# A gated encoder block on one core: the latent columns move from plain groups of pieces to block products, and three one-tile gate pieces stand beside each attention head

## The reference, cut to what matters

```python
u = rmsnorm(x, g_mix)
z = u @ w_in      # columns: qa 1024 | ka 256 | va 256 | cq 512 | ckv 512 | kr 64 | ga 2048 | gb 2048
oa = attention(rope(rmsnorm(qa)), rope(rmsnorm(ka)), va)        # 8 heads of 128, 2 key/value heads
qb = rmsnorm(cq) @ w_q_b                                        # branch B starts from the latents
kv = rmsnorm(ckv) @ w_kv_b
ob = attention([q_nope, rope(q_pe)], [k_nope, rope(kr)], vb)    # 8 heads
merged = sigmoid(ga) * (oa @ w_a_out) + sigmoid(gb) * (ob @ w_b_out)
h = x + merged @ w_o
h = h + (silu(g_) * u_) @ w_down                                # SwiGLU, 5632 wide
h = h + sigmoid(rmsnorm(h) @ w_ple_gate) * rmsnorm(p @ w_ple_proj)
out = rmsnorm(h)
```

## Time and profile before

| | us |
|---|---|
| median of 3 runs | 2646.98 |
| lowest and highest | 2646.76, 2647.21 |
| span of the profiled execution | 2645.5 |
| PE busy in it | 2630.8 |
| DVE busy | 2019.1 |
| ACT busy | 1284.6 |

### The profile page before, as it was taken

How to read it: one execution, slowest core, us unless ns; L and a number is a source line. 1 busy time by engine, 2 the same in 40 slices (tenths; PEclk the granted TensorE clock), 3 DMA queues, 4 the chain that set the end, 5 groups by cost and what they waited for, 6 DMA issues and landing times.

```text
span 2645.5 us, 37943 instructions
## 1 busy us (share of the span) xinstructions
PE 2630.8 (99%) x14980; PEld 2307.9 (87%) x14980; DVE 2019.1 (76%) x2314; ACT 1284.6 (49%) x1609; POOL 178.6 (7%) x140
## 2 busy tenths in 40 slices
PE   9999999999999999999999999999999999999998
PEld 7989888888888888898888888888899898999887
DVE  8887777655565433488998999999899898898745
ACT  7545455434455233455545555554555353454543
POOL 0000000010000111100000000000000000000052
PEclk9999999999999999999999999999999999999999
DMA  7545423233333554446546555545666664653332
GB/s 252 154 143 169 123 87 96 80 91 119 98 100 103 183 210 124 145 127 177 166 144 178 168 158 173 175 138 166 175 198 213 211 211 140 207 140 106 94 101 99
DMA packets 135791, 392.75 MB, mean 148 GB/s; under 512 B 11600, under 2 KB 41424, under 8 KB 133072
## 3 DMA queue, kind: packets, MB, share of 16 engines
q1 hardware_dynamic: 119904, 342.27, 38.8%
q0 software_dynamic: 11232, 39.85, 8.5%
q10 hardware_dynamic: 4496, 8.44, 0.8%
HBM read 304.26 MB, written 46.40 MB: 133 GB/s over the span
## 4 chain that ended last, share of the span: by engine, by line
PE 97%; DVE 2%; ACT 1%; issue 0%; DMA 0%; DVEq 0%; ACTq 0%
PE ps L1218 23%; PE ps L848 23%; PE ps L1224 16%; PE ps L853 11%; PE ps L1220 4%; PE ps L1221 4%; PE ps L997 3%; PE ps L1003 3%; PE ps L837 1%; PE ps L835 1%; PE ps L836 1%; PE ps L918 1%; PE ps L1000 1%; PE ps L999 1%; PE ps L1250 1%; PE ps L907 0%
## 5 line engine op out<-in xcount | busy, mean ns | idle before, releaser
L1311 ACT ACTIVATE w_hi<-raw 128x1024 fp32r<-128x1024 f32 (+1 forms) x538 | 562.6, 1046 | 753.5 <-PE ps L1224 409.9
L848 PE MATMUL ps<-arena,w_hi 128*128 128x512 f32 x2704 | 647.6, 391 | 0.2 <-DVE res L2038 0.2
L848 PEld LDWEIGHTS ps<-arena,w_hi 128*128 128x128 f32 x2704 | 505.3, 188 | 108.7 <-issue 3.4
L1218 PE MATMUL ps<-arena,w_hi 128*128 128x512 f32 x1792 | 448.7, 392 | 0.0
L2586 DVE TENSOR_TENSOR w_lo<-raw,w_hi 128x1024 fp32r<-128x1024 f32 (+1 forms) x314 | 373.8, 1191 | 78.8 <-ACT w_hi L1311 77.3
L2026 DVE TENSOR_TENSOR w_lo<-raw,w_hi 128x1024 fp32r<-128x1024 f32 x172 | 219.1, 1275 | 224.5 <-ACT w_hi L1311 223.6
L1218 PEld LDWEIGHTS ps<-arena,w_hi 128*128 128x128 f32 x1792 | 322.3, 189 | 57.6
L1224 PEld LDWEIGHTS ps<-arena,w_lo 128*128 128x128 f32 x2468 | 332.3, 191 | 17.5
L1224 PE MATMUL ps<-arena,w_lo 128*128 128x256 f32 x2468 | 346.4, 283 | 0.0
L853 PE MATMUL ps<-arena,w_lo 128*128 128x512 f32 x1352 | 334.3, 389 | 0.0
L1311 ACT ACTIVATE hi<-raw 128x1024 fp32r<-128x1024 f32 (+1 forms) x182 | 189.6, 1042 | 243.4 <-PE ps L1224 212.8
(11 more groups left out here) (280 smaller groups left out, 3360.0 us busy)
## 6 DMA issues: line engine op xcount, KB each, us to landing
raw<-w_gu SPq DMA_DIRECT2D x174, 512.0 KB, 4.1
raw<-raw POOLq DMA_DIRECT2D x70, 512.0 KB, 7.7
raw<-w_in SPq DMA_DIRECT2D x68, 512.0 KB, 3.6
raw<-w_dn SPq DMA_DIRECT2D x64, 512.0 KB, 5.3
hid<-res SPq DMA_DIRECT2D x22, 1024.0 KB, 5.0
raw<-w_z SPq DMA_DIRECT2D x40, 512.0 KB, 5.4
raw<-w_o SPq DMA_DIRECT2D x32, 512.0 KB, 3.7
raw<-w_pg SPq DMA_DIRECT2D x32, 512.0 KB, 3.6
```

Of the source, the lines that this page charges most:

```text
L848: mm(ps[:, bank + t, :], w_hi[:, s, t, k], x[:, part, :], start=first and k == 0 and part == 0, stop=False)
L1218: mm(parts, w, x[:, :, k], start=fresh and k == 0, stop=False, skip_group_check=not fresh)
L1311: return nc.scalar.activation(out, in_, ACT.Copy, scale=scale)
```

## The change

- The latents' four column groups become four more units of block products (14 units; five wide pairs instead of three). SP stores their results in `lat_dram` and loads them back during the heads.
- The gates that stand beside the heads are done as twelve single column tiles, two pieces each (8 contraction tiles by 1 column tile, `gate_piece`), in banks 0, 2, 3. Each of the eight heads has three such pieces instead of four old ones.
- The values' products (`weigh`) move: the first two come after 12 of the third piece's 16 high matmuls, the last two after 4 of its 8 low ones.
- ACT scales the probabilities in attention A too (`exps_scaled`), which DVE did. Sigmoids of these gates come in five batches of two or three tiles instead of one for each group.
- The latents' squares are taken from the loaded tiles in heads 6 and 7 and behind them; both totals stand in the group of last gates. The rotated key is made later. The loops over heads are unrolled. The seam's pieces use the other slot of high parts.

```diff
+            def gate_piece(p, among_hi=None, among_lo=None):
...
+                for k in range(8):
+                    if among_hi:
+                        among_hi(k)
+                    w, x = w_hi[:, s, k // KP, k % KP], u_tile(8 * (p % 2) + k)
+                    mm(out, w, x[:, 0, :], start=first and k == 0, stop=False)
+                    mm(out, w, x[:, 1, :], start=False, stop=False)
...
+            def gqa_head(h):
+                kv = h // GROUP
                 score(h, [Q_A], [K_A[kv]], h + 5)
...
+                gate_piece(3 * h)
+                if h < HEADS - 1:
                     head_total(h + 3)
...
+                gate_piece(3 * h + 1)
                 turn_p(h, 0, PT_BANK)
                 turn_p(h, 1, PT_BANK)
...
+                def first_weighs(k):
+                    if k == 6:
+                        weigh(h, 0, V_A[kv], PT_A)
+                        turn_p(h, 2, PT_BANK)
+                        turn_p(h, 3, PT_BANK)
+                        weigh(h, 1, V_A[kv], PT_A)
...
                 def last_weighs(k):
-                    if k == 3:
+                    if k == 4:
                         weigh(h, 2, V_A[kv], PT_A)
                         weigh(h, 3, V_A[kv], PT_A)
...
+                gate_piece(3 * h + 2, first_weighs, last_weighs)
...
+            pe.wait_ge(emptied, G_GATE + 9)
+            for j in range(4):
+                piece(N_LAST_GATES + j, j, 2, u_pieces(j), j == 0, j == 3)
+                if j == 0:
+                    pe.wait_ge(o_lo, HEADS)
+                    total(1, 6)
+                if j == 2:
+                    total(2, 7)
```

On ACT (first part) and DVE (second part):

```diff
+            def gate_sigmoids(b):
+
+                first, last = max(3 * b - 1, 0), 3 * b + 2
+                t = tmp[:, gate_row(first):3, :]
+                act.wait_ge(emptied, G_GATE + min(last, 13))
                 nc.scalar.activation(t, t, ACT.Sigmoid).then_inc(gate_sig, 1)
...
+            def gqa_head(h):
+                b = 3 * h
+                exps_scaled(h)
+                whi(N_GATE + b + 2, (b + 2) % 4)
+                if h < HEADS - 1:
                     head_root(h + 3)
...
+                if h in (1, 3, 5):
+                    gate_sigmoids(h // 2)
+                    ln_exp_table()
                 pt_split(h, 0, PT_A)
                 pt_split(h, 1, PT_A)
...
+            def gqa_head(h):
+                b = 3 * h
                 softmax(h)
-                wlo(b + 2, 2)
-                if more:
+                if h % 2:
+                    gate_tile(b // 2)
+                wlo(N_GATE + b + 2, (b + 2) % 4)
+                if h < HEADS - 1:
+                    tile = res[:, h + 1:h + 2, :]
                     head_norm(h + 3, tile, G_QN)
                     dve.wait_ge(hnorm, h + 4)
...
                 pt_split(h, 0, PT_A)
                 pt_split(h, 1, PT_A)
...
+            dve.wait_ge(kv_lat_in, 16)
+            recip(1, 1, 6, 2, LORA)
             wlo(N_LAST_GATES + 2, 2)
+            key_latent(0)
+            key_latent(1)
+            wlo(N_LAST_GATES + 3, 3)
+            key_latent(2)
+            key_latent(3)
             sum_low(2)
```

More of the change, by code:

```diff
@@ L401, in total_bank @@
         def total_bank(m):
[L402 removed]
+            return 0 if m == 1 else 1
         def z_operand(v, j):
@@ L1024, in _ @@
             in_group(G_SEAM + 1, {1: [lambda: head_total(2)]}, N_SEAM + 4, 2)
-            def gqa_head(h, kv, more, bank=2):
-                b = h * 4 + N_GATE
-                score(h, [Q_A], [K_A[kv]], h + 5)
[L1029 to L1032, removed]
-                if more:
+            def gate_piece(p, among_hi=None, among_lo=None):
+                n, s, i, first = N_GATE + p, p % HL, p // 2, p % 2 == 0
+                out = ps[:, FILL_BANK[i], :]
+                if first:
+                    if i == 0:
+                        pe.wait_ge(hnorm, 2)
+                    elif i < 3:
+                        pe.wait_ge(emptied, G_GATE)
+                    elif i == 10:
+                        pe.wait_ge(hnorm, HEADS + KV_HEADS)
+                    else:
+                        pe.wait_ge(emptied, G_GATE + (i - 1 if i == 11 else i - 2))
+                pe.wait_ge(w_hi_done, n + 1)
+                for k in range(8):
[4 more added lines that the diff above has]
+                    mm(out, w, x[:, 1, :], start=False, stop=False)
+                pe.wait_ge(w_lo_done, n + 1)
+                for k in range(8):
+                    if among_lo:
+                        among_lo(k)
+                    w, x = w_lo[:, s, k // KP, k % KP], u_tile(8 * (p % 2) + k)
+                    m = mm(out, w, x[:, 0, :], start=False, stop=not first and k == 7)
+                m.then_inc(piece_used, 1)
@@ L1047, in last_weighs @@
                         weigh(h, 3, V_A[kv], PT_A)
-                piece(b + 3, 3, bank, u_pieces(3), False, True, before=last_weighs)
-            gqa_head(0, 0, True)
-            with pe.Fori(1, GROUP) as h:
-                gqa_head(h, 0, True)
-            with pe.Fori(GROUP, HEADS - 2) as h:
-                gqa_head(h, 1, True)
-            gqa_head(HEADS - 2, 1, True)
-            gqa_head(HEADS - 1, 1, False, 0)
-            def u_group(n, j0, group, step=None):
-                free(group)
-                for j in range(4):
-                    piece(n + j, j0 + j, 2 * (group % 2), u_pieces(j), j == 0, j == 3)
-                    if step and j == 1:
-                        step()
@@ L1650, in exps_scaled @@
[L1650 to L1663 removed]
+            gate_sigmoids(4)
```

366 lines of the change are left out of this document (170 added, 196 removed).

## The result

The changed kernel takes **2663.47 us** (median of 4, 2663.06 to 2664.07) against 2646.88 (2646.76 to 2647.21): a ratio of 1.0062, 95% interval 1.0048 to 1.0077. It is slower, by 16.6 us. The forecast was 2659.0 with a range of 2650 to 2666. The profiled execution has a span of 2662.3 us, 16.8 more than before.

What follows compares the result with a forecast made beforehand. PE bounds the kernel, busy 2630.8 of 2645.5 us. Span: 2645.5 - 9.2 (PE's work) + 13.3 (heads) + 5.9 (latents) + 2.0 (clock) = 2657.5; the median lies 1.5 above, so 2659.0 us, range 2650 to 2666.

Steps and rivals of the forecast that it cites:

- PE's work: Whole kernel: 28 wide products add 78.2 us, sixteen pieces removed save 87.0, head 0's old wait saves 0.4; sum -9.2.
- The heads' chain: Heads 0 to 6: PE waits for DVE's transposed tile at the first value product; 13.3 us in all, restarts included.
- restart: At every wait of PE: 0.16 us charged beyond the idle time shown.
- the mildest bound: Heads: with ACT's scaling costing nothing, the tile is still 0.4 us behind PE; with head 0 the waits make 5.
- The latents' wait: At the second latent total: operands ready at T + 22.5, PE there at T + 16.8; 5.7 us, with restart 5.9.
- ACT's delay: Behind the first latent total: ACT has other work ahead, so the logarithm comes about 0.8 us later.
- That order on DVE has not changed: Latents: the 15.68 us from first total to end of last low part, taken from the kernel before, still hold.
- The clock behind it: Behind the latents' wait: PE restarts at the lower clock, costing 0 to 3.1 us, taken as 2.0.
- is then early enough: Behind the latents' wait: the last gates' low parts and rotated key come in time, PE being held up by 5.7 us.
- Loads and the table loads' drain: Rival: two load waits of 3 us give 2665, chance 0.1; drain of 1.38 us per table load gives 2667, chance 0.03.
- Nothing on PE: Heads 1, 3, 5: ACT's sigmoid batches and table loads lie beside the chain and cost PE nothing.
- Behind branch B: From branch B's first transposing call to the program's end: a change of 0 us.

Runs made afterwards that it cites:

- the filled wait: The changed kernel with 28 more matmuls of 512 columns, their result unread, ahead of the second latent's total, where PE idles: 2659.53 us.
- the new order: The changed kernel with the first two transposed tiles' splits ahead of the rotation, the other two ahead of the rotated query's split, on DVE and ACT: 2649.95 us.

## Why the prediction was right, and where it was short

- **PE's work, -9.2.** Right to 0.3: +78.6 for the units 0.4 of it more than forecast, -87.0 for the pieces, -0.5 for head 0's old wait.
- **The heads' chain.** Right in its place, its releaser and its size, with 0.16 of restart for each wait: waits of 2.87, 1.28 to 1.31 and 1.56 where 2.9, 1.4 and 1.7 were forecast; head periods of 25.63 and 25.87 where the forecast was 25.6 and 25.9. The run in which DVE scales gave the 0.4 us of the mildest bound. One place was missed: in head 6 part of the wait stands ahead of the third piece (0.73), for the norm on the same chain. Head 7 lasts 23.6 instead of 24.0, since it has no square total (0.45), and head 0 28.8 instead of 27, for the next point's reason.
- **The term that was mis-sized in the heads: the clock.** The prediction charged a lower clock to the latents' wait alone. In the profiled execution it also fell at head 0's 2.87 us, and 1.7 us of the missing 4.8 are that. Five other traces with the same wait don't have it. The four runs of the changed kernel lie within 1.0 us of each other, less than 1.7, which speaks for the same fall in more than the profiled one; no trace shows it, so what part it has in the median of 2663.47 stays open.
- **The latents' wait, 5.9.** Measured 7.0, made of three differences that partly cancel, so 5.9 is nearer than its terms. ACT's delay was forecast as 0.8 and is 0.4 (the logarithm 1.47 us after the total instead of 1.06). The step that failed is "That order on DVE has not changed", from which the sum took over its duration of 15.68: the order has not changed, but GpSimd's additions now fall among it, and the run without them gives 1.96 us back. PE itself comes 0.46 later than the sum had it: the piece behind the first total takes 4.08 us from its first row to its low part instead of 3.63, as it did before the change, and the sum charged 5.44 for it. In all -0.4 + 1.96 - 0.46 = 1.1.
- **The clock behind it, 2.0.** Measured 2.8 in this execution, 2.66 by the run with the filled wait; of the bounds 0 to 3.1 the upper one was the nearer. The choice of 2.0 between them rested on no row of a restart in the middle of the program.
- **What comes behind "is then early enough".** True only because PE was held up, as that sentence said; the run that moved the total alone shows 7.15 us of waits hidden under those 7.0.
- **Loads and the table loads' drain.** Neither came. PE has no wait for DMA, and the wide products kept their pace of 2.79 us. The instruction behind a table load starts 0.01 us behind its end (600.77, and 470.76 in head 3 above). "Nothing on PE" holds for the changed kernel, where a longer chain hid the batches; with the new order the batches of three tiles cost 0.26 us in heads 3 and 5, the one of two tiles nothing.
- **Behind branch B, forecast 0.** Measured 0.9, of which 0.63 is one idle time of PE at 1154.08 us, for a high part on ACT. Before, the same matmul (1137.37) has none. In the kernels above it varies from none (the filled wait) to 0.54, and its cause stays open.

## What to carry to other kernels

When work is taken out of the engine that bounds the time, the work that stays loses its cover: add up the chain on the other engines against the shorter cover before counting the gain, and plan to reorder those queues in the same change. Moving the one instruction that waits is not enough where everything behind it in the queue is late too; put the short operations that the bounding engine needs next ahead of the long ones that it doesn't. Price an idle time of PE with its clock: in the one place where it fell after 2.35 us of waiting, the wait cost 4.2.

## What was not expected of the hardware

- Idle times of PE between 2.35 and 3.5 us lowered the clock in some executions and not in others: 2.87 us in one trace of six, 3.48 us not and 2.35 us yes within one execution. It fell in each of the five traces that have an idle time of 4.87 us or more (4.87, 5.60 and three of 6.8), and cost 1.6 to 2.8 us of slow matmuls.
- Two additions of 128x512 on GpSimd (3.00 us together) made one DVE operation of 0.69 us take 1.67 and the next, of 1.23, take 2.19.
